# First layer of a two-layer encoder step: input rows scaled in place on GpSimd and transposed plainly, instead of turned through a scaled diagonal

## What is computed

```python
def rms_norm(x, g):
    y = xf * lax.rsqrt(jnp.mean(xf * xf, axis=-1, keepdims=True) + EPS)
    return (y * g.astype(jnp.float32)).astype(x.dtype)

def trunk_layer(x, c, pos, w_ada, b_ada, g_pre, w_in, w_out, g_post, past):
    mod = jax.nn.silu(c) @ w_ada + b_ada
    shift, scale, gate = jnp.split(mod, 3, axis=-1)
    h = rms_norm(x, g_pre) * (1.0 + scale[:, None, :]) + shift[:, None, :]
    q_a, k_a, v_a, gate_a, q_i, k_i, w_i, q_b, k_b, v_b, gate_b = split_cols(h @ w_in)
    ...                                  # sparse attention with an indexer, retention
    y = rms_norm(mixed @ w_out, g_post)
    x = x + gate[:, None, :] * y
```

## Time and profile before

| | |
|---|---|
| median of three runs | 1437.32 us (1437.22 to 1438.34) |
| span of the profiled execution | 1434.8 us |
| PE busy | 1389.2 us |
| DVE busy | 1008.5 us |
| ACT busy | 784.4 us |
| POOL busy | 405.2 us |

### The profile page before, as it was taken

One profiled execution on the slowest core, in us unless ns is written; L12 is line 12 of the kernel. 1 busy time (PEld: TensorE's weight loads), 2 busy tenths in 40 slices (PEclk: granted clock), 3 DMA queues, 4 the chain that ended last, 5 costly groups with the idle time before them and its releaser, 6 DMA issues.

```text
span 1434.8 us, 24595 instructions
## 1 busy us (share of the span) xinstructions
PE 1389.2 (97%) x7687; PEld 1065.3 (74%) x7687; DVE 1008.5 (70%) x2983; ACT 784.4 (55%) x1916; POOL 405.2 (28%) x382
## 2 busy tenths in 40 slices
PE   6999999999999999999998999999999999999997
PEld 2865777888887677668877577878888766766886
DVE  0687889999996545542398789999999654555225
ACT  2555666666326665664454566666632566666432
POOL 3741333443331011001287124443343100100100
PEclk9999999999999999999999999999999999999999
DMA  9743333302232112213252111211223211222325
GB/s 314 232 135 100 94 122 110 83 23 60 58 90 66 43 39 69 81 65 105 88 181 69 41 32 44 59 40 43 62 58 90 66 34 46 69 65 67 112 74 176
DMA packets 125190, 122.05 MB, mean 85 GB/s; under 512 B 33256, under 2 KB 94024, under 8 KB 125064
## 3 DMA queue, kind: packets, MB, share of 16 engines
q1 hardware_dynamic: 124608, 120.36, 27.7%
q10 hardware_dynamic: 456, 0.13, 0.0%
HBM read 93.55 MB, written 26.90 MB: 84 GB/s over the span
## 4 chain that ended last, share of the span: by engine, by line
PE 57%; DVE 31%; issue 5%; POOL 3%; DMA 2%; ACT 2%; DVEq 0%; ACTq 0%; SPq 0%; POOLq 0%
DVE U L1787 11%; PE proj L1016 10%; PE proj L1017 10%; PE proj L1019 9%; PE turn L995 9%; PE logit L1043 7%; PE out_bank L1070 5%; PE spare L1043 2%; DVE turned L1742 2%; DVE by_cos_sin L1727 2%; DVE by_cos_sin L1725 2%; DVE probsT_more L1860 2%; DVE probsT_more L1864 1%; POOL h_lo L1565 1%; PE spare L981 1%
## 5 line engine op out<-in xcount | busy, mean ns | idle before, releaser
L1016 PE MATMUL proj<-w_hi,h_hi 128*128 128x512 f32 (+2 forms) x1440 | 574.6, 399 | 0.8 <-POOL h_lo L1565 0.4
L1017 PE MATMUL proj<-w_lo,h_hi 128*128 128x512 f32 (+2 forms) x1440 | 535.5, 372 | 0.0
L1019 PE MATMUL proj<-w_hi,h_lo 128*128 128x512 f32 (+2 forms) x1280 | 477.7, 373 | 0.0
L1559 POOL TENSOR_TENSOR w_lo<-w_raw,w_hi 128x512 fp32r<-128x512 f32 (+2 forms) x160 | 202.4, 1266 | 745.6 <-ACT w_hi L1265 745.4
L1016 PEld LDWEIGHTS proj<-w_hi,h_hi 128*128 128x128 f32 x1440 | 272.1, 189 | 50.7 <-issue 15.1
L1017 PEld LDWEIGHTS proj<-w_lo,h_hi 128*128 128x128 f32 x1440 | 272.3, 189 | 31.0
L1019 PEld LDWEIGHTS proj<-w_hi,h_lo 128*128 128x128 f32 x1280 | 240.5, 188 | 37.1
L1787 DVE TENSOR_SCALAR_CACHE_REDUCE U<-score,cand 128x384 bf16<-128x384 f32 x310 | 223.0, 752 | 2.2
L1043 PE MATMUL logit<-keys,queries 64*128 64x512 f32 (+4 forms) x454 | 137.2, 542 | 2.3 <-ACT U L1408 1.6
L1388 ACT ACTIVATE probsT_more<-turn 128x512 f32<-128x512 f32 (+3 forms) x156 | 76.1, 491 | 95.8 <-PE turn L995 95.6
L995 PEld LDWEIGHTS turn<-ident,U 128*128 128x128 f32 x584 | 65.9, 140 | 52.1 <-issue 37.0
(11 more groups left out here) (206 smaller groups left out, 2131.8 us busy)
## 6 DMA issues: line engine op xcount, KB each, us to landing
w_raw<-in_w_in_dram SPq DMA_DIRECT2D x80, 256.0 KB, 3.2
probsT_more<-in_w_ada_dram SPq DMA_DIRECT2D x64, 256.0 KB, 3.7
score<-mixed_dram SPq DMA_DIRECT2D x36, 256.0 KB, 3.0
score<-in_w_ada_dram SPq DMA_DIRECT2D x32, 256.0 KB, 5.0
w_raw<-in_w_out_dram SPq DMA_DIRECT2D x32, 256.0 KB, 3.4
U<-in_x_prompt_dram SPq DMA_DIRECT2D x12, 512.0 KB, 4.1
mixed_dram<-U SPq DMA_DIRECT2D x24, 192.0 KB, 2.1
gates_dram<-U SPq DMA_DIRECT2D x18, 256.0 KB, 2.0
```

Of the source, the lines that this page charges most:

```text
L1016: nc.tensor.matmul(out, h_hi[:, k, tile], hi, start=(k == 0), stop=False)
L1017: ins = nc.tensor.matmul(out, h_hi[:, k, tile], lo, start=False, stop=(t == SAMPLE and k == KT - 1))
L1019: ins = nc.tensor.matmul(out, h_lo[:, k, tile], hi, start=False, stop=(k == KT - 1))
L1559: nc.gpsimd.tensor_tensor(w_lo[:, s % WS, 0:w], w_raw[:, n % RAWS, 0:w], w_hi[:, s % WS, 0:w].bitcast(F32), ALU.subtract).then_inc(w_lo_re ...
```

## The change

A function `scaled_rows(l, t)` is true for the first layer's tiles 2 to 8. For these, POOL's third instruction in `input_diagonal` no longer multiplies the 128 x 128 identity by the inverse root, but the tile's rows themselves, in place, over all 1024 columns. PE then transposes the eight blocks with the identity. Tiles 0 and 1 and the second layer stay as they were. POOL's wait for the turn of tile t - 2 (which guarded the diagonal's two slots) falls away in the first layer; it had none to guard for rows. No instruction changes its place in any engine's order.

```diff
+        def scaled_rows(l, t):
+            return l == 0 and t >= 2
...
                     for b in range(4):
                         k = 4 * u + b
-                        ins = nc.tensor.matmul(turns.bank(key)[:, b * P:(b + 1) * P],
-                                               xt(l * NT + t)[0:n, k * P:(k + 1) * P], diagonal(l, t)[0:n, :],
-                                               start=True, stop=True)
+                        if scaled_rows(l, t):
+                            ins = nc.tensor.transpose(turns.bank(key)[:, b * P:(b + 1) * P],
+                                                      xt(t)[:, k * P:(k + 1) * P], ident[:])
+                        else:
+                            ins = nc.tensor.matmul(turns.bank(key)[:, b * P:(b + 1) * P],
+                                                   xt(l * NT + t)[0:n, k * P:(k + 1) * P], diagonal(l, t)[0:n, :],
+                                                   start=True, stop=True)
...
             def input_diagonal(l, t):
                 s, n = t % 2, diagonal_ordinal(l, t)
+                m = tokens(t)
...
-                if t >= 2 and turned_raw(l, t - 2):
+                pool.wait_ge(input_rooted, n + 1)
+                if scaled_rows(l, t):
+                    nc.gpsimd.tensor_scalar(xt(t)[0:m, :], xt(t)[0:m, :], input_root[0:m, s, :], None,
+                                            ALU.mult).then_inc(diagonal_ready, 1)
+                    return
+                if l and t - 2 in RAW_TILES:
                     turns.wait_full(pool, ("h", l, t - 2, 1))
-                pool.wait_ge(input_rooted, n + 1)
                 nc.gpsimd.tensor_scalar(diagonal(l, t), ident[:], input_root[:, s, :], None,
                                         ALU.mult).then_inc(diagonal_ready, 1)
```

## The result

The changed kernel took 1447.76 us in the median of five runs (1446.67 to 1448.02), the kernel before 1437.22 us beside it (1436.3 to 1438.34). The ratio is 1.0071, 95% interval 1.0059 to 1.0083: slower by 10.5 us. The profiled execution has a span of 1444.9 us against 1434.8, which is 10.1 more. 1448.2 us had been forecast.

A forecast was written before the change was run, and what follows sets the result against it. POOL's queue was taken to bound the kernel from 44 to 62 us. Scaling delay 10.49, PE's turns -0.3, DVE 0.2 and PE's clock 0.5 made 10.9 us on 1437.3, so 1448.2 us; range 1445.9 to 1451.6, widened to 1443 to 1453.5.

The forecast's parts named there:

- Who bounds the start of the projections: First layer, 44 to 62 us: projections start by POOL's remainder, so PE's 7.1 us saving there mostly makes PE wait.
- The price of the scaling: POOL's scaling over 1024 columns: 2963 ns against 621, so 2.34 us more per tile, bounds 2.23 to 2.46.
- The three delays: Remainders of tiles 1, 2 and 3 on POOL, behind the added scalings: late by 4.68, 7.02 and 9.17 us.
- Where the growth ends: At tile 4's remainder the delay reaches 10.49 us and stays there; POOL runs without a pause until about 85 us.
- PE's clock: Idle time ahead of projections 1 to 4 lowers PE's granted clock: 0.5 us taken, bounds 0 and 2.1.
- PE's turn at tile 7: Shorter turn ahead of tile 6's projection, where PE itself was last: -0.3 us.
- tile 8's turn: Shorter PE turn of tile 8: put at nothing, 1.0 us if it gave all it has.
- DVE beside POOL: Two-input DVE instruction slowed beside POOL's scaling, bare in tile 4's step: 0.2 us, bounds 0 and 1.1.
- The sum: All terms for the whole kernel: 10.49 - 0.3 + 0.2 + 0.5 = 10.9 us, giving 1448.2 us.
- A check that was wrong: Sign to look for over the whole span: PE's busy time falls by some 7 us while the span grows.
- The Trainium skill's price: Rival for the first layer's scaling: about 1.5 us each, delay about 3.5 us, 1440.8 us; chance 6%.

The follow-up runs named there:

- pe_part_alone: Changed kernel with plain transposes kept, but the rows not scaled and POOL making unread diagonals again: 1436.25 us, ratio 0.9995 to the kernel before.
- pool_part_alone: Changed kernel with POOL's scaling kept, but PE turning rows by a matmul with the unscaled identity: 1446.81 us, ratio 1.0069 to the kernel before.
- unread_pool_work: Kernel before, plus two 256-column POOL instructions with unread output behind each diagonal of tiles 2 to 8: 1445.38 us, ratio 1.0059.
- act_scales: Changed kernel with rows scaled on ACT, and POOL's tile remainder ahead of the weights' remainder: 1435.88 us, ratio 0.9994 to the kernel before.
- act_scales_high_first: ACT-scaling kernel with ACT's high part of a later tile ahead of the query and key copies: 1436.2 us, ratio 0.9995 to the kernel before.

## Why the prediction was right

It was right in the time, 1448.2 against 1447.76, and in the mechanism. Some of its terms were too high, and that the medians still came within 0.4 us of it is in part luck, as the sum below shows.

- **Who bounds the start of the projections.** Right, and shown by the two halves alone: taking 7 us from PE was worth 0.7 at most (`pe_part_alone`), and giving it back to PE cost nothing that the times show (`pool_part_alone`). The added work on POOL alone makes the loss (`unread_pool_work`), and nearly all of it is gone when the work stands on another engine (`act_scales`, which has the remainders in a better order too).
- **The price of the scaling.** 2.34 us more had been taken from the median of line 1619, with a lower bound of 2.23. It was 2.24 (2.862 against 0.621). The price was at its lower bound, since the median of the second layer's rows had included three of about 3.07. On top of it 0.07 us of a gap ahead of each instruction went away. The three delays, forecast as 4.68, 7.02 and 9.17, were 4.45, 6.47 and 8.46.
- **Where the growth ends.** Right: at tile 4. POOL's first pause came ahead of tile 4's remainder, at 75.8 us, where the forecast had it at about 85. POOL would have been free for its remainder at 74.51 + 1.28 = 75.79 us, 9.6 late, where 10.49 had been forecast.
- **PE's clock.** For tile 4 0.4 us had been put bare. The granted clock was 0.52 and 0.63 from 70 to 74 us, in tile 3's projection, and tile 4's remainder waited 0.38 us for ACT behind it. Without the low clock ACT would have been there at 66.18 + 8.46 = 74.64, an estimate; so its way was 1.5 us late, near the 1.7 that had been worked out for one fall, and POOL's order would have decided. Of the 1.7 us that a fall in tile 4's step could have cost, nothing came: from 74 us on the clock stood at 1.00. The term of 0.5 was 0.4. No run takes the clock away by itself, so that ACT was late through the clock is read from the order of events and not tested.
- **PE's turn at tile 7.** -0.3 forecast, 9.99 to 9.68 measured. At tile 8's turn nothing came, as taken: tile 7's projection, right behind it, is late by 9.69 (97.26 and 106.95).
- **DVE beside POOL.** 0.2 us forecast, none came. In tile 4's step DVE's second half of tile 5 ended at 83.46 and ACT took it at 84.55, 1.1 us later. The two-input instruction ahead of it (at 81.56) took 0.62 us, although POOL's scaling was under way from 80.11 to 82.97; in the kernel before it took 1.43 (at 71.16). So the lengthening that the earlier trace rows show beside a scaling was not repeated here. A one-input instruction ahead of it was longer by 0.42 us, and the slack covered that.
- **The sum.** At 107 us the trace has 9.7, and 10.1 at the end of the span; the medians are 10.5 apart. Against 9.7 the forecast, 10.9, was too high by 0.9 in POOL's part (0.5 by the price, 0.4 by the gaps), 0.2 in DVE's and 0.1 in the clock's. The 0.8 us between 9.7 and the medians' 10.5 have no term in it. The ratio's interval, 8.5 to 11.9 us, holds both, so they may be scatter; they hide most of the error, and this is the luck in the result.
- **A check that was wrong.** PE's busy time was to fall by 7 us over the whole span. It fell by 4.0, and by 4.4 in `pe_part_alone` (1384.8), with nothing added to POOL. From 40 to 110 us it did fall by 7.1 in that run (68.89 to 61.81), as the turns should have it; from 0 to 40 and from 700 to 800 us, where nothing was changed, it was 1.3 and 1.4 higher. So the total of one execution is no check of a few us here. In the changed kernel the matmuls under the low clock from 50 to 56 and from 70 to 74 us last longer as well, and the page counts them as busy.

The Trainium skill's price in "GPSIMD Engine Reference", section 3.1, an estimate of 1.5 us for the scaling, would have given a loss of 3.5 us. The instruction took 2.86 and the loss was 10.5. Where page and trace differ, the trace decides.

## What to carry to other kernels

An engine's share of the span says nothing about the place where its work is put. Before work is moved from the busiest engine to an idle one, look at what stands behind the new place in that engine's queue, and whether it starts with or without idle time ahead of it. Starts at one constant distance behind another engine's instruction tell who holds them, even where the trace shows no idle time; here taking 7 us from the other candidate bore it out. And where such a queue is found, its order is the cheaper thing to change: putting the two remainders first gained 1.8 us with not one instruction more or less. But work that comes last in one iteration still stands ahead of the next, and the loads that wait for POOL's work have to be followed too.

## What the runs showed of the hardware

- POOL's multiplication of a tensor by a column took 0.62 us for 128 columns, 0.93 for 256 (`unread_pool_work`), 1.58 for 512 and 2.86 for 1024. That is about 2.5 ns for each column and 0.3 us besides, in place or not. On ACT a copy with such a scale took 1.15 us for 1024 columns (`act_scales`). The last tile has 64 rows and took as long as 128 (2.86): the rows that are left out save nothing.
- An instruction of DVE with one input in SBUF, 384 columns by a column, took 0.87 us while POOL's scaling ran (at 80.57 us of the changed kernel) and 0.45 in the kernel before. One of 512 columns took 1.18 (at 89.67) and 0.51. I had looked for such lengthening in instructions with two inputs only, and one of these, at 81.56, wasn't lengthened by the same scaling.
- A two-input instruction of DVE over 512 columns took 1.84 us when it began together with POOL's subtraction (84.22 and 84.24 in `act_scales_high_first`), and 0.75 when it was nearly done by then (83.79 and 84.49 in `act_scales`).
- The granted clock was 0.90 in the stretch of 2 us in which PE's idle time began and 0.50 in the next, and it was still 0.50 when PE took up work again at 52.29. It rose while PE was working.
